# Scan stage: next front loads first on the sync queue, block-level evictions ahead of the constant copy and the decays on ScalarE

## The reference, cut to what matters

```python
def step(S, inp):
    r_t, w_t, k_t, v_t, kk_t, kka_t = inp
    sa = jnp.einsum('bdhvk,bdhk->bdhv', S, kk_t)
    S = (S * w_t[..., None, :] - sa[..., :, None] * kka_t[..., None, :]
         + v_t[..., :, None] * k_t[..., None, :])
    return S, jnp.einsum('bdhvk,bdhk->bdhv', S, r_t)
s_final, ys = lax.scan(step, s0.astype(f32), xs)
```

## Time and profile before

| what | value |
|---|---|
| median of 3 runs | 4147.47 us (4143.14 to 4159.44) |
| the profiled execution: its own time | 4145.14 us |
| its span in the profile | 4143.3 us |
| mean granted clock of TensorE, as a share of full speed | 0.944 |
| busy PE / DVE / ACT / POOL in the span | 3663.0 / 1207.4 / 748.9 / 1186.2 us |
| the scan in the span | about 1022 to 2053 us |

### The profile page before, as it was taken

One profiled execution on the slowest core, in us unless ns is written; L12 is line 12 of the kernel. 1 busy time (PEld: TensorE's weight loads), 2 busy tenths in 40 slices (PEclk: granted clock), 3 DMA queues, 4 the chain that ended last, 5 costly groups with the idle time before them and its releaser, 6 DMA issues. The chain is left out here.

```text
span 4143.3 us, 63261 instructions
## 1 busy us (share of the span) xinstructions
PE 3663.0 (88%) x24883; PEld 2853.4 (69%) x24884; DVE 1207.4 (29%) x2276; ACT 748.9 (18%) x1399; POOL 1186.2 (29%) x1712
## 2 busy tenths in 40 slices
PE   8799999996688989889799999999999927999960
PEld 1566666664688888888689898898988913444430
DVE  0122222222344444444212212122121231222227
ACT  0122222221232223222111111111111101111113
POOL 0133333333555655566210111101111031000013
PEclk9899999998799999999899999999999968999985
DMA  6522222222233223332260111101111134675226
GB/s 244 206 86 86 88 82 81 81 77 107 77 97 96 65 85 97 98 93 69 81 234 34 44 57 39 62 34 44 57 39 62 39 104 164 237 254 189 93 102 213
DMA packets 273319, 424.40 MB, mean 102 GB/s; under 512 B 123100, under 2 KB 174020, under 8 KB 273094
## 3 DMA queue, kind: packets, MB, share of 16 engines
q1 hardware_dynamic: 250616, 348.23, 25.0%
q0 software_dynamic: 13040, 43.54, 3.2%
q10 hardware_dynamic: 9444, 29.30, 1.8%
HBM read 287.98 MB, written 133.02 MB: 102 GB/s over the span
## 5 line engine op out<-in xcount | busy, mean ns | idle before, releaser
L1692 PE MATMUL c_ps<-c_hT,c_wg 128*128 128x128 f32 x6528 | 752.8, 276 | 25.1 <-DMA c_wg<-in_w_in 25.1
L1692 PEld LDWEIGHTS c_ps<-c_hT,c_wg 128*128 128x128 f32 x6528 | 744.0, 193 | 33.0 <-issue 29.5
L640 PE MATMUL a_ps<-a_win,a_hT 128*128 128x512 f32 (+1 forms) x1088 | 416.2, 540 | 3.6 <-DVE a_mix L560 3.4
L2121 PE MATMUL e_ps<-expert_up,e_xT 128*128 x784 | 347.4, 596 | 2.3 <-DVE e_xT L2083 2.3
L634 PE MATMUL a_ps<-a_hT,a_win 128*128 128x128 f32 x2992 | 344.1, 277 | 1.6 <-ACT a_hT L384 1.6
L634 PEld LDWEIGHTS a_ps<-a_hT,a_win 128*128 128x128 f32 x2992 | 340.9, 193 | 5.6 <-issue 2.7
L640 PEld LDWEIGHTS a_ps<-a_win,a_hT 128*128 128x128 f32 x1088 | 204.0, 190 | 199.8 <-issue 187.0
L1036 POOL TENSOR_TENSOR b_tmp<-b_tt,b_ta 128x126 f32<-128x126 f32 (+22 forms) x527 | 202.2, 384 | 325.8 <-DMA b_ta<-s_a 269.2
L2121 PEld LDWEIGHTS e_ps<-expert_up,e_xT 128*128 128x128 f32 x784 | 149.3, 191 | 191.8 <-issue 191.8
L1692 PE MATMUL c_ps<-c_wo,c_mT 128*128 128x512 f32 x544 | 236.3, 592 | 0.0
L1039 POOL TENSOR_TENSOR b_tt<-b_tt,b_tmp 128x126 f32<-128x126 f32 (+22 forms) x527 | 213.3, 405 | 41.3
(11 more groups left out here) (301 smaller groups left out, 5246.2 us busy)
## 6 DMA issues: line engine op xcount, KB each, us to landing
expert_up<-in_exp_w SPq DMA_DIRECT2D x32, 1024.0 KB, 9.9
s_D<-a_oD SPq DMA_DIRECT2D x34, 768.0 KB, 6.0
b_f<-s_D SPq DMA_DIRECT2D x34, 768.0 KB, 7.6
s_yr<-e_yo ACTq DMA_DIRECT2D x49, 512.0 KB, 3.1
m_w<-in_ada_w SPq DMA_DIRECT2D x12, 2048.0 KB, 7.9
b_f<-s_A SPq DMA_DIRECT2D x34, 512.0 KB, 5.8
expert_down<-in_exp_w SPq DMA_DIRECT2D x16, 1024.0 KB, 12.2
s_A<-a_oA SPq DMA_DIRECT2D x17, 768.0 KB, 3.4
```

The costliest lines, as they stand in the source:

```text
L640: ins = nc.tensor.matmul(ps[:, bank, 0:width], hT[b][:, k, :], win[:, k, c:c + width], start=k == 0, stop=k == KD - 1)
L1692: return nc.tensor.matmul(out, lhsT, rhs, start=start, stop=stop)
L2121: return nc.tensor.matmul(out, lhsT, rhs, start=start, stop=stop)
```

## The change

In SP's step the wait and the issue of the front loads of tile q+2 move from behind the v loads to the first place, ahead of `inverse_in(q)`. In ACT's step the four evictions of the block level move ahead of `identity(q+1)` and `own_decay(q+2)`. Nothing is added or taken away.

```diff
+                    if left > 1:
+                        for d in range(2):
+                            sp.wait_ge(const_in, 48)
+                            after(sp, k_ok[d], q + 1)
+                            after(sp, b_ok[d], q + 1)
+                            after(sp, pm_ps[d], q + 1)
+                            load_front(two[d], d)
                     inverse_in(q)
                     for d in range(2):
                         if not first:
@@
                             load_v(one[d], d, 1 - b)
-                    if left > 1:
-                        for d in range(2):
-                            sp.wait_ge(const_in, 48)
-                            after(sp, k_ok[d], q + 1)
-                            after(sp, b_ok[d], q + 1)
-                            after(sp, pm_ps[d], q + 1)
-                            load_front(two[d], d)
                     if left > 0:
                         diagonal_out(q + 1)
@@
                     if left > 0:
                         raw(q + 1)
+                    for d, g in GROUPS:
+                        after(act, u5_ps[d][g], q)
+                        a(flat(U[d][:, heads(g), :]), bank(d, 2 * g), ACT.Copy).then_inc(u5_ok[d][g], 1)
+                    if left > 0:
                         identity(q + 1)
                     if left > 1:
                         for d in range(2):
                             own_decay(q + 2, d)
-                    for d, g in GROUPS:
-                        after(act, u5_ps[d][g], q)
-                        a(flat(U[d][:, heads(g), :]), bank(d, 2 * g), ACT.Copy).then_inc(u5_ok[d][g], 1)
```

## The result

The changed kernel took 4277.62 us (median of 4, 4275.74 to 4281.54) against 4151.68 us before (median of 4 in the same comparison): a ratio of 1.03, 95% interval 1.0275 to 1.0325. The forecast was 4286 us, 4212 to 4340.

The account below looks back on a forecast made before the run. The prediction took the scan as nearly bound by PE before, and a circle of POOL, SP and DVE as the bound after: 15 x (67.2 - 57.83) = +141 us on 4145.1 us gave 4286 us, range 4212 to 4340.

Parts of the forecast that it names:

- 1, 2: T to the store of the inverse: POOL's blocks(q) and scaled(q+1), 11.35 us, then issuing the second pair of front loads on SP, 1.13 us.
- T: Clock of a step: end of POOL's inverse for tile q; periods between were 57.83 us before, forecast 67.2 us.
- Step 3: SP's store of the inverse must land before its reload: 4.3 us plus 4.1 us behind front loads, sum 8.4 us.
- 4, 5: reload to the diagonal stores: From the first `b_tz` load through DVE's turning, 6.5 us, then DVE turning the raw matrices, 1.31 us.
- 6: diagonal stores to the next T: Diagonal stores to the end of POOL's next inverse: 38.5 us with front loads landed, 44.0 us at the range's end.
- the slow circle: POOL's inverse, SP's store and reload, DVE's turning, diagonal stores, next inverse: 67.2 us a period, PE not in it.
- the hold: Delay of the inverse's store by 2.5 MB of front loads ahead on its queue: 4.1 us, bounds 0 and 4.1.
- The estimate from the 358 GB/s: Front loads land in 7.3 us, so the inverse's store is not held: 4224 us; rival's chance 0.17.
- the tail: Behind T(15) no front load is issued and the order is that of before, so no change was added.
- the second circle: POOL's inverse, SP's store and reload, DVE's turning, diagonal stores and load: beside PE, not the bound before, some slack.
- the value of the evictions: Early ACT evictions end PE's stall for `b_u`: 0 to 70.5 us, at most 115 with clock; nothing reaches the end.
- What the profile after was to show: T to T about 67 us, `b_tt` store 12.5 us after T, PE waiting some 14 us a step at block level.

Follow-up runs that it names:

- the best order: Against the kernel with only the evictions early: SP issues inverse, front loads, diagonal blocks, then y stores and v loads; 4085.86 us, ratio 0.9841 to the kernel before.

## Why the prediction was right

Step by step, forecast against step 7 of the changed kernel:

| step of the forecast | forecast, us | measured, us |
|---|---|---|
| 1, 2: T to the store of the inverse | 12.5 | 12.61 |
| 3: store to reload | 8.4 | 7.46 |
| 4, 5: reload to the diagonal stores | 7.8 | 7.88 |
| 6: diagonal stores to the next T | 38.5 | 38.48 |
| period | 67.2 | 66.43 in this step, 67.03 in the mean |

In step 7 of the kernel before, the same four were 0.02, 5.10, 12.44 and 40.30 us, 57.86 together (T = 1494.86, store 1494.88, reload 1499.98, diagonal stores 1512.42, next T 1552.72). So 12.6 us of waiting and a return 2.4 us longer added only 8.6 us. Before, the diagonal stores had waited for PE's raw matrices; in the slow circle these are there in time, which gives 4.6 us back, and 1.8 more come back between the diagonal stores and the next T.

The main claim, that the signal for the front loads comes after the inverse in POOL's program and so drags the store of the inverse behind it, is shown three ways: SP's part alone has the whole loss, the wait without its loads keeps it, and giving the signal 6.25 us sooner takes 5.93 us off the period.

Step 3, the one with bounds far apart, was 0.9 us too long. The store was held: 7.46 us behind the loads, 3.55 without them ahead. So the hold itself, 3.9 us, was forecast well (4.1), and most of the error is the return without a hold, 3.55 us where I had taken the middle of two steps, 4.3. That the mean of the period comes out within 0.2 us is in part luck: over steps 1 to 13 of the changed kernel the four terms average 12.63, 7.53, 7.84 and 38.87 us, so a short third step and a long last one offset each other. The estimate from the 358 GB/s of the Trainium skill ("DMA: Bandwidth & Descriptors", section Specifications) had the hold vanish and would have given 4224 us; the store's own return decides against it here. The Trainium skill, "DMA: Bandwidth & Descriptors", section "Queues, rings and completion order", has the transfers of one queue start in order on each DMA engine, and the held store agrees; no run showed one overtaking.

The profiled execution took 4275.74 us, 10 below the forecast. The period accounts for 15 x (67.2 - 67.03) = 2.6 of it. Two terms were not in the sum. From T(15) to T(16) the changed kernel took 50.43 us, before 54.38, 4.0 less: I had left the tail at nothing, but PE, which has some 12 to 15 us of room a step in the slow circle, enters it ahead, and the diagonal stores of the last tile go out 12.7 us after T(15) (2090.02 to 2102.76) instead of 15.9 (1955.53 to 1971.38). And in the profiled execution T(0) came 3.6 us earlier than before; the change does not touch what lies ahead of it.

One reading was too generous: that the second circle "has some slack" beside PE. The slack was about one us: with PE's stall gone the period fell from 57.83 only to 56.76. The same rows that gave me the hold in step 3 had it: the diagonal stores stood right behind the front loads before the change too. For this change it decided nothing, since the circle became the bound anyhow; for the value of the evictions it did (26 us, not 70.5 or more).

What the profile after was to show came as said, but for one thing: PE's wait, 12.0 to 14.8 us in steps 1 to 14, is there, listed as "issue" and not with DVE or the loads.

## What to carry to other kernels

A wait moved ahead in an engine's queue delays all that stood behind it, so before moving a command find out when its signal is given, in the order of the engine that gives it: here POOL gives it only after the inverse that the front loads were moved ahead of. A stall of the busiest engine is worth only as much as the next circle leaves: follow store, reload and small transfers from one period to the next before counting the stall as gain. And in a shared DMA queue look at what must land soon and what merely has to land: the 1% between the evictions alone and the best order came with putting 1 MB that nobody awaited behind 32 KB blocks on which the next inverse waited.

## What the runs showed of the hardware that I had not expected

After PE had waited 5.5 and 1.1 us for the fronts, it was granted 0.50 of its clock from 1534 until 1550 us, 16 us in all, the last 10 of them without any gap. After the 12.4 us wait at the block level in the changed kernel the low stretch was short, as this window of the changed kernel and the next show:

```profile
1578.60:1583.00 4.40, 4.36 (x22) 4.39 (x23) 3.02 (x5) 1.16 (x2) 0.00 (x0) 0.53 0.74 237
1583.00:1600.00 17.00, 16.89 (x176) 15.22 (x175) 6.83 (x10) 8.41 (x16) 6.77 (x19) 1.00 0.25 50
```

With the evictions alone, PE waited only 1.85 us for the fronts and 1.34 us for ACT, and soon behind them stood these 12 us without a gap at a granted clock of 0.60:

```profile
1505.00:1517.00 12.00, 12.00 (x67) 12.00 (x67) 2.89 (x6) 1.19 (x2) 9.58 (x26) 0.60 0.01 1
```

So shorter waits cost more clock than a longer one. Which work follows differs (products of 128 rows and columns after the long wait; after the short ones four wide products and then products of 64 rows or columns); which property of it decides was not tried. The other thing is in the run with the loads behind the diagonal blocks: DVE's last products `b_shd` of a step took 1.4 to 1.5 us beside POOL's `scaled`, and 0.4 to 0.5 us in the steps in which `scaled` came after them.
